# Weight buffers of a decoder trunk moved to addresses of their own modulo 512 bytes

## The reference

```python
h = rms_norm(x, mix_norm[l])
z = h @ w_in[l]
...
x = x + m @ w_out[l]
h = rms_norm(x, ffn_norm[l])
f = swiglu(h, ...) if l % 2 == 0 else moe_swiglu(h, router_w[i], ...)
x = x + f
```

## Time and profile before

| | us |
|---|---|
| median of 3 runs | 1451.75 |
| lowest and highest run | 1451.59, 1453.03 |
| span of the profiled execution | 1453.1 |
| TensorE busy in it | 1426.3 |
| VectorE busy | 1179.7 |
| ScalarE busy | 884.7 |

### The profile page before, as it was taken

One profiled execution on the slowest core, in us unless ns is written; L12 is line 12 of the kernel. 1 busy time (PEld: TensorE's weight loads), 2 busy tenths in 40 slices (PEclk: granted clock), 3 DMA queues, 4 the chain that ended last, 5 costly groups with the idle time before them and its releaser, 6 DMA issues.

```text
span 1453.1 us, 22261 instructions
## 1 busy us (share of the span) xinstructions
PE 1426.3 (98%) x8381; PEld 1202.9 (83%) x8381; DVE 1179.7 (81%) x1181; ACT 884.7 (61%) x879; POOL 141.4 (10%) x195
## 2 busy tenths in 40 slices
PE   8999999999999999999999999999999999999997
PEld 6887888999998888887888888888888888888875
DVE  7998886676467697876988988889898898898896
ACT  5334754534344345644768768777777777777774
POOL 1910100000000000101960000000000000000100
PEclk9999999999999999999999999999999999999999
DMA  7443445776455442454999999999999999999993
GB/s 285 136 180 121 156 159 189 261 246 233 151 189 192 174 160 97 151 188 161 365 413 390 406 363 399 380 364 413 353 398 394 354 404 370 379 397 347 419 376 145
DMA packets 94247, 408.87 MB, mean 281 GB/s; under 512 B 28769, under 2 KB 43233, under 8 KB 47714
## 3 DMA queue, kind: packets, MB, share of 16 engines
q1 hardware_dynamic: 75984, 391.37, 69.9%
q10 hardware_dynamic: 17042, 12.36, 2.6%
q0 software_dynamic: 1152, 4.19, 0.7%
HBM read 390.98 MB, written 14.16 MB: 279 GB/s over the span
## 4 chain that ended last, share of the span: by engine, by line
PE 78%; DVE 11%; DMA 3%; SPq 3%; issue 2%; ACT 2%; POOL 1%; DVEq 0%; POOLq 0%; ACTq 0%
PE psum L1938 25%; PE psum L1940 24%; PE psum L1939 24%; DVE w_lo L605 4%; SPq L696 3%; PE psum L1954 2%; DMA w_raw<-in_stream 2%; DMA x_normed<-y_rows,row_number 1%; ACT w_hi L599 1%; ACT square_out L993 0%; PE psum L2284 0%; PE psum L2005 0%; DVE s_r L1511 0%; ACT prob L1129 0%; PE psum L1987 0%
## 5 line engine op out<-in xcount | busy, mean ns | idle before, releaser
L605 DVE TENSOR_TENSOR w_lo<-w_raw,w_hi 128x2048 fp32r<-128x2048 f32 x267 | 607.9, 2293 | 130.2 <-ACT w_hi L599 129.4
L599 ACT ACTIVATE w_hi<-w_raw 128x2048 fp32r<-128x2048 f32 x267 | 509.4, 1915 | 251.1 <-PE psum L1940 191.5
L1938 PE MATMUL psum<-w_hi,hsT_hi 128*128 128x512 f32 x448 | 176.0, 393 | 0.8 <-DVE hsT_lo L1829 0.8
L1940 PE MATMUL psum<-w_lo,hsT_hi 128*128 128x512 f32 x448 | 174.5, 390 | 0.0
L1939 PE MATMUL psum<-w_hi,hsT_lo 128*128 128x512 f32 x448 | 174.3, 389 | 0.0
L1938 PE MATMUL psum<-w_hi,hT_hi 128*128 128x512 f32 x376 | 152.7, 406 | 1.8 <-ACT gate_ssm L1075 1.4
L605 DVE TENSOR_TENSOR w_lo_more<-w_raw,w_hi_more 128x2048 fp32r<-128x2048 f32 x56 | 128.2, 2289 | 24.3 <-ACT w_hi_more L599 23.6
L1940 PE MATMUL psum<-w_lo,hT_hi 128*128 128x512 f32 x376 | 147.4, 392 | 0.0
L1939 PE MATMUL psum<-w_hi,hT_lo 128*128 128x512 f32 x376 | 147.1, 391 | 0.0
L599 ACT ACTIVATE w_hi_more<-w_raw 128x2048 fp32r<-128x2048 f32 x56 | 107.1, 1913 | 21.6 <-DMA w_raw<-in_stream 12.4
L1938 PE MATMUL psum<-hT_hi,w_hi 128*128 128x256 f32 x416 | 116.6, 280 | 0.2 <-DVE hT_lo L1463 0.2
(11 more groups left out here) (429 smaller groups left out, 2651.2 us busy)
## 6 DMA issues: line engine op xcount, KB each, us to landing
w_raw<-in_stream SPq DMA_DIRECT2D x323, 1024.0 KB, 6.9
w_raw_more<-in_stream SPq DMA_DIRECT2D x40, 1024.0 KB, 7.7
h_rows<-one_row ACTq DMA_DIRECT2D x10, 512.0 KB, 6.6
round_rows<-h_rows SPq DMA_DIRECT2D x7, 512.0 KB, 7.0
y_rows<-y_slots ACTq DMA_DIRECT2D x7, 512.0 KB, 9.2
y_rows<-one_row ACTq DMA_DIRECT2D x4, 512.0 KB, 6.2
gain_row<-in_gain_rows SPq DMA_DIRECT2D x3, 512.0 KB
x_tok<-in_x SPq DMA_DIRECT2D x2, 512.0 KB, 6.2
```

The lines of the kernel that those rows point to most:

```text
L599: nc.scalar.activation(split_of(seg, i)[0], raw_of(seg, i), ACT.Copy).then_inc(s_hi, 1)
L605: nc.vector.tensor_tensor(l_, raw_of(seg, i), h.bitcast(F32), ALU.subtract).then_inc(s_lo, 1)
L1938: mm(out, lh, rh, start=start, stop=False)
L1940: return mm(out, lh, rl, start=False, stop=stop)
```

## The change

The places of the rings no longer begin at offset 0. A moving weight slot in the high ring begins 16, 48 or 80 floats (64, 192, 320 bytes) past its place's old start, in the low ring 8, 48 or 112 floats (32, 192, 448 bytes). The further buffers of the rounds begin 256 (`w_hi_more0`), 384 (`w_lo_more0`), 32 (`w_hi_more1`) and 128 bytes (`w_lo_more1`) off. Stationary slots of FFN keep their 192 bytes. The three mixer slots of a layer whose weights stand in the array, and FFN's u0, aren't called stationary in the code and take the new offsets of their places. The raw buffers, the activations' tensors and all instructions stay as they were; tensors that lie between `w_lo` and the next padding (the identity, the masks, small tables) move by 256 bytes modulo 512.

```diff
 LEAD = 48
+HI_LEAD, LO_LEAD = (16, 48, 80), (8, 48, 112)
+MORE_LEAD = (32, 128, 256, 384)
...
-        wh = sb("w_hi", [P, NW * SLOT + LEAD], F32R)
+        wh = sb("w_hi", [P, NW * SLOT + HI_LEAD[-1]], F32R)
         here[0] += (a_hT - here[0]) % 512
-        wl = sb("w_lo", [P, NW * SLOT + LEAD], F32R)
+        wl = sb("w_lo", [P, NW * SLOT + LO_LEAD[-1]], F32R)
...
-        a_rr = room(16384)
+        a_rr = room(16384 + 512)
...
-        whx = [at("w_hi_more0", [P, 1, SLOT], F32R, a_rr), at("w_hi_more1", [P, 1, SLOT], F32R, a_tab + 16384)]
-        wlx = [at("w_lo_more0", [P, 1, SLOT], F32R, a_rr + 8192), at("w_lo_more1", [P, 1, SLOT], F32R, a_tab + 24576)]
+        whx = [at("w_hi_more0", [P, 1, SLOT], F32R, a_rr + MORE_LEAD[2]), at("w_hi_more1", [P, 1, SLOT], F32R, a_tab + 16384 + MORE_LEAD[0])]
+        wlx = [at("w_lo_more0", [P, 1, SLOT], F32R, a_rr + 8192 + MORE_LEAD[3]),
+               at("w_lo_more1", [P, 1, SLOT], F32R, a_tab + 24576 + MORE_LEAD[1])]
...
             p = i % NW if seg < 3 else ROUND_POS[i]
             if p < NW:
-                a = (p + 2) % NW * SLOT + (LEAD if stationary(seg, i) else 0)
-                return wh[:, a:a + SLOT], wl[:, a:a + SLOT]
+                m = (p + 2) % NW
+                ah, al = (m * SLOT + (LEAD if stationary(seg, i) else lead[m]) for lead in (HI_LEAD, LO_LEAD))
+                return wh[:, ah:ah + SLOT], wl[:, al:al + SLOT]
             return whx[p - NW][:, 0, :], wlx[p - NW][:, 0, :]
```

## The result

| | before | after |
|---|---|---|
| median, us | 1452.26 (4 runs, 1451.59 to 1453.03) | 1467.09 (4 runs, 1465.31 to 1468.16) |
| ratio, 95% interval | | 1.0097 [1.0085, 1.011] |
| span of the profiled execution | 1453.1 | 1463.5 |
| that execution's own time | not given | 1465.31 |

The change costs 14.8 us, 1% (12.3 to 16.0 us by the interval). The forecast was slower by 6.3 us: the direction and the range held, the size was less than half of what came.

The account below looks back on a forecast made before the run. The prediction took TensorE's number of products times the step between starts as the bound. Its terms, 6.9 - 0.6 = +6.3 us with the others at 0, added to the median of 1451.75 gave 1458 us, range 1436 to 1476.

Parts of the forecast that it names:

- What bounds the kernel: Whole kernel: TensorE, busy 98% of the span, sets the time by products times step, with the granted clock full throughout.
- Term 1: VectorE's and ScalarE's splits: addresses make no difference, times stay at 2293 and 1915 ns, 0 us.
- Term 4: Transposes and small tables, which move 256 bytes: 0 us, their count being small beside 4848.
- Term 2: The 4848 moving products: late steps after slot starts cost 13.8 us, of which half is taken, +6.9 us.
- the nine steps: 512-column products after an interruption: some nine steps until 226.7 ns returns, 4.6 ns more each meanwhile.
- The upper end of the term: Moving products: no slot settles, 4848 x 4.6 ns = +22 us.
- The 2 us that the range adds for 32 bytes: Top of the range: 2 us for slots read from 32 bytes off, added to +22 us.
- Term 3: The mixers' 288 products with standing weights: step 117.8 instead of 120.0 ns, -0.6 us.
- The small form of the faster rival: FFN: 18 slots behind moved down slots (864 products) fall into 113.4 instead of 117.8 ns, -3.8 us, 1448.
- the slower one: Whole kernel, the forecast itself: products lose the steady rate, by itself 1455 to 1476 us, chance 0.45.
- Faster: Moving products: equal offsets are the bad relation, every place away gains; 1441 at -2.2 ns, 1420 at -6.6; chance 0.35.
- No change: TensorE's operands don't meet and run history sets the rates, or only 256 columns feel offsets; 1451 or so, chance 0.20.

Follow-up runs that it names:

- the map: Two survey kernels, each place at its own offset, high and low parts alike: 1466.73 and 1475.25 us, against 1452.83 and 1452.33 for the kernel before.

## Why the prediction was right and wrong

**What bounds the kernel**: right. TensorE stays at 98% and no other engine, load or wait takes its place. Only "full throughout" of the clock was too much: the stage's mean of 0.98 hid a stretch of FFN at the half clock (below).

**Term 1, the splits, 0**: right (2294 and 1918 ns; 2293 and 1915 before). **Term 4**: nothing in the trace speaks against 0.

**Term 2, the moving products, +6.9 us: the step that failed.** Its direction held: equal addresses have a steady step of 226.7 ns, and moved places lose it. Its mechanism held only in part. It took 226.7 for what any undisturbed row at one relation falls into, priced the late steps behind each slot's start, and took half of that, because "a change need not cost the nine steps" from u0 to g1. That treats the new relation as a disturbance which passes. But the kernel with all places at 192 has one relation and no such disturbance, and still settles at 233.4: what is lost is not the way back to 226.7 but the rate itself, at every step. Nor are nine late steps the rule behind an interruption: before's own means in the rounds, 226.9 to 227.4, lie at most 0.7 ns above 226.7. The upper end of the term (no slot settles, 4.6 ns each) had the size: measured 4.3 ns, so 4848 x 4.3 = +21 us. That was luck, for the 4.6 came from steps behind transposes at offset 0, which the change did not touch. (The trace has 4872 moving products; the 24 of the first slot, worth 0.1 us, were not counted.) My aside that place 1 would keep one relation, both parts at 192, was true and helped nothing: it is the slowest of the five. The 2 us that the range adds for 32 bytes rest on no row; the map has 233.1 ns there, no more than at 192.

**Term 3, the mixers' standing weights, -0.6 us**: about half of it. Place 0 stayed (119.7 and 119.8 ns), place 1 (192 bytes) went from 119.6 to 117.8, 192 products or -0.3 us.

**The small form of the faster rival came true inside the slower one.** FFN's slots behind a moved down slot fell into 113.4: the steps of 256 columns in all of FFN sum to 120.4 us instead of 123.6, -3.2 us (I had named -3.8).

**The sum.** +21.0 for the moving products and -3.5 for all products of 256 columns (1344 x -2.6) are +17.5; the medians say +14.8, the interval at most 16.0. Part of the rest is seen in the trace: the late steps (those left out of the means) of the rounds cost 1.5 us less. That slower products leave loads and splits more time would explain it; no run tried that by itself.

The two spans differ by 10.4 us only, and there the clock accounts for the gap. Windows of the kernels before and after in FFN (columns as in the earlier trace rows); then TensorE's last product of u7 and its first of g8, before and after:

```profile
386.00:391.00 5.00, 5.00 (x30) 3.56 (x29) 1.23 (x2) 0.38 (x1) 0.00 (x0) 0.50 0.07 8
...
385.00:390.00 5.00, 5.00 (x34) 3.85 (x33) 1.43 (x2) 0.39 (x1) 0.00 (x0) 1.00 0.11 13
```

```profile
382.03 0.28 PE L1940 MATMUL psum<-hT_lo,w_hi 128*128 128x256 f32 x1
...
395.28 0.28 PE L1938 MATMUL psum<-hT_hi,w_hi 128*128 128x256 f32 x1
...
381.23 0.28 PE L1944 MATMUL psum<-hT_lo,w_hi 128*128 128x256 f32 x1
...
391.40 0.28 PE L1942 MATMUL psum<-hT_hi,w_hi 128*128 128x256 f32 x1
```

Before, the granted clock fell to 0.50 (1.2 GHz) behind a row of small products (64*64, 16 columns), and d6 began at 427 ns a product; after, it stayed at 1.00 behind the same row. From u7 to g8 that is 13.25 us against 10.17, 3.1 us. In mixer 0 the half-clock stretch of the earlier trace rows costs 1.4 us in the same way (the same products take from 56.48 to 71.18 us before, from 56.32 to 69.63 after), and the first eight products of the first slot, some of them at 427 ns before and none after, 0.9 us (3.11 against 2.18 us). 17.5 - 1.5 - 3.1 - 1.4 - 0.9 = 10.6, beside 10.4 measured. This differs from execution to execution: the other three of the kernel after had mean granted clocks of 0.994 to 0.996, against 0.998 in the profiled one, and took 1.8 to 2.9 us longer. So the profiled execution after lay below its kernel's median. That before lay above its own, and "nothing of weight lies around" that span was off: eleven of the twelve profiled executions since have an own time 1.7 to 2.0 us above their span, which would put the one before at about 1455 (an estimate), not at the median. So the medians are the fairer measure, and of FFN's gain of 5.5 us the clock made 3.1.

**The rivals.** *Faster*: 512 columns have no better relation than 0 and 256 among the twelve tried. *No change*, by which 113.4 against 117.8 is only history and the operands never meet: its first half is right, by the kernel that moved the down slots alone; its second is refuted by 1475.6 against 1452.72, one relation at 192 against everything moved together. The Trainium skill ("SBUF — State Buffer", "Who interferes with whom") says that TensorE never waits on anyone. In these runs no other engine stands in its way either, but it loses 23 us of 1453 by where its own two operands lie, and there the measurement decides. The gap that the Trainium skill gives ("TensorE: Matmul & The Clock Gate", "Back-to-back issue gap"), columns over 2.4 GHz plus about 2.5 ns, is 215.8 ns for 512 columns, an estimate by that page's formula. No relation here reached it; 226.7 was the best.

**What stays open**: why 0 and 256 bytes are good for 512 columns and all others tried are not, why it is the other way round for 256 columns, and what in the run ahead chooses between 113.4 and 117.8.

## What to carry to other kernels

Where every product loads a tile of its own and streams 512 columns past it, put both at the same address modulo 512 bytes, or 256 apart; at the other offsets tried this kernel paid 3 to 7 ns a product of 227, up to 1.6% of its time. Don't carry this over to shorter products: with 256 columns and standing weights, 0 and 256 bytes were the slow offsets (u0 at 120.0 in the kernel before, 119.9 with all at 256), 64 gave 113 to 116 in u0 and the mixers. Read the step from start to start in an undisturbed stretch and by buffer, since a mean duration (396 against 393) shows little of it. And when a rate has been lost, ask first whether it comes back by itself: give the whole kernel the new condition and look, before taking half.

## What was unexpected of the hardware

- The difference of the addresses counts and the addresses don't: everything moved by 192 bytes gives 1.000, the streaming side alone 1.0155.
- 256 bytes are as good as 0, and alternating between them with every product is free (226.7), while 192 settles at 233.4.
- A slot's rate is inherited: in the kernel with only the further buffers moved, a slot at a good relation ran at 231 for all its products behind one at 32 and 128 bytes; in FFN the same products at the same addresses run at 113.4 or 117.8 for 18 slots, by where the slots between them lie.
- The settled steps are multiples of 6.67 ns, over one step or three: 113.3 is 17 of them, 120.0 is 18, 226.7 is 34, 233.3 is 35, and three steps of 117.8 are 53. That is a pattern in the numbers; no run tested what lies behind it.
